# RG-LRU steps issued two at a time, with a ring of four convolution buffers, in a hybrid decoder trunk

## The reference

```python
u = conv_b; u = u + xc[:, j:j+L] * conv_w[j]          # causal convolution, j = 0..3
r  = sigmoid(u @ w_a + b_a); ig = sigmoid(u @ w_i + b_i)   # block-diagonal weights
log_a = LRU_C * r * log_sigmoid(lam)
a  = exp(log_a)
bt = sqrt(-expm1(2 * log_a)) * ig * u
h_t = a_t * h_{t-1} + bt_t                            # scan along the sequence
o_lru = h_seq * gelu(gate)
```

## Time and profile before

| | us |
|---|---|
| median of the 2 runs shown | 4967.77 |
| the two runs | 4776.38 and 5159.16 |
| the profiled execution | 4762.55 |
| its span on the slowest core | 4761.5 |
| spans of the 8 cores in it | 4717.6 to 4761.5 |

### The profile page before, as it was taken

One profiled execution on the slowest core, in us unless ns is written; L12 is line 12 of the kernel. 1 busy time (PEld: TensorE's weight loads), 2 busy tenths in 40 slices (PEclk: granted clock), 3 DMA queues, 4 the chain that ended last, 5 costly groups with the idle time before them and its releaser, 6 DMA issues.

```text
span 4761.5 us, 61283 instructions; the slowest of 8 cores (4717.6 to 4761.5 us)
## 1 busy us (share of the span) xinstructions
PE 3698.8 (78%) x18520; PEld 1598.8 (34%) x18520; DVE 1870.8 (39%) x3170; ACT 1877.3 (39%) x3420; POOL 1318.3 (28%) x1687
## 2 busy tenths in 40 slices
PE   5578976579965799757895778976798778976797
PEld 2223432234422244322342223422243223422243
DVE  3544146441354512454413543146413543146413
ACT  4553236442264521455322552246412552246411
POOL 2503125121243211350312413134212413134212
PEclk9768988579986799866897868987798868987798
DMA  5214421224223054220444204422142304522143
GB/s 109 30 28 65 70 44 27 38 36 70 43 49 47 6 82 61 41 29 10 68 69 113 37 13 73 73 36 33 29 76 46 55 11 73 74 36 33 29 76 78
DMA packets 178574, 239.80 MB, mean 50 GB/s; under 512 B 76880, under 2 KB 79440, under 8 KB 178000
## 3 DMA queue, kind: packets, MB, share of 16 engines
q0 software_dynamic: 129312, 205.77, 28.6%
q1 hardware_dynamic: 48944, 30.12, 2.5%
HBM read 431.16 MB, written 18.51 MB: 94 GB/s over the span
## 4 chain that ended last, share of the span: by engine, by line
PE 58%; DVE 12%; ACT 10%; issue 8%; POOL 7%; DMA 4%; ACTq 0%; DVEq 0%; SPq 0%; POOLq 0%
PE P L345 50%; DVE arena L464 3%; POOL x L382 3%; PE P L692 3%; DVE tmpa L380 3%; PE P L361 2%; ACT sq L359 2%; DVE act L372 1%; DMA arena<-cache_v 1%; ACT arena L700 1%; POOL arena L499 1%; ACT arena L660 1%; DMA x<-xT_in 1%; DVE arena L487 1%; POOL tmpb L609 1%
## 5 line engine op out<-in xcount | busy, mean ns | idle before, releaser
L345 PE MATMUL P<-act,wsl 128*128 128x512 bf16 (+1 forms) x11520 | 2235.0, 358 | 120.6 <-ACT tmpb L608 58.1
L345 PEld LDWEIGHTS P<-act,wsl 128*128 128x128 bf16 x11520 | 1027.6, 102 | 1322.6 <-issue 320.3
L905 DVE TENSOR_TENSOR H<-P,tmpb 128x512 bf16<-128x512 f32 (+1 forms) x440 | 262.0, 601 | 1305.8 <-PE P L345 1138.6
L382 POOL TENSOR_TENSOR x<-x,tmpa 128x512 f32<-128x512 f32 (+1 forms) x320 | 390.3, 1238 | 1282.1 <-DVE tmpa L380 1097.7
L345 PE MATMUL P<-H,wsl 128*128 128x512 bf16 (+1 forms) x3520 | 644.8, 346 | 14.4 <-DMA wsl<-w_down_u 14.4
L903 ACT ACTIVATE tmpb<-P 128x512 f32<-128x512 f32 (+1 forms) x440 | 231.2, 525 | 1006.9 <-PE P L345 1006.8
L361 PE MATMUL P<-sq,ones 128*128 128x512 bf16 (+1 forms) x720 | 290.9, 446 | 363.3 <-ACT sq L359 344.9
L345 PEld LDWEIGHTS P<-H,wsl 128*128 128x128 bf16 x3520 | 302.5, 99 | 349.6 <-issue 22.7
L380 DVE SCALAR_TENSOR_TENSOR tmpa<-F,prm_sb,rstd 128x512 f32<-128x512 f32 (+1 forms) x320 | 287.8, 933 | 256.6 <-POOL x L382 127.2
L464 DVE SCALAR_TENSOR_TENSOR arena<-F,prm_sb,arena 128x512 f32<-128x512 f32 (+1 forms) x240 | 266.2, 1109 | 196.0 <-ACT arena L461 178.0
L359 ACT ACTIVATE sq<-F 128x512 bf16<-128x512 f32 (+1 forms) x400 | 193.5, 548 | 338.3 <-PE P L361 199.9
(11 more groups left out here) (134 smaller groups left out, 3252.9 us busy)
## 6 DMA issues: line engine op xcount, KB each, us to landing
wsl<-w_gate_u POOLq DMA_DIRECT2D x176, 256.0 KB, 4.1
wsl<-w_up_u POOLq DMA_DIRECT2D x176, 256.0 KB, 4.8
wsl<-w_down_u POOLq DMA_DIRECT2D x128, 352.0 KB, 4.8
wsl<-w_in_u POOLq DMA_DIRECT2D x168, 256.0 KB, 4.6
wsl<-w_out_u POOLq DMA_DIRECT2D x64, 256.0 KB, 4.3
x<-xT_in SPq DMA_DIRECT2D x32, 256.0 KB, 12.8
yT<-x SPq DMA_DIRECT2D x16, 512.0 KB, 2.8
sk_old<-cache_k SPq DMA_DIRECT2D x4, 992.0 KB, 7.4
```

Of the source, the lines that this page charges most:

```text
L345: S.op("pe", lambda e, lt=lt, rh=rh, j=j: e.matmul(out_ap, lhsT=lt, rhs=rh, start=(j == 0), stop=(j == n - 1)), reads=rk, writes=[out_key] ...
L382: S.op("pool", lambda e: e.tensor_tensor(x[:, c, lo_:hi_], x[:, c, lo_:hi_], tmpa[j][:, 0:n], ALU.add), reads=akeys("x", [c], s, lo_, hi_) ...
L905: S.op("dve", lambda e: e.tensor_tensor(H[:, c, lo_:hi_], P[bu_][:, 0:n], tmpb[j][:, 0:n], ALU.mult), reads=[pk(bu_), ("tmpb", j)], writes ...
```

## The change

`u32` and `u16` get a fourth buffer. `lru_A` loses its square root, which becomes a function of its own, `lru_S`, and can leave out the cast of the next step. `lru_advance` issues two steps in one call, ahead of every third slot, with `lru_B` of a step ahead of `lru_A` of the step two later. Ahead of the first slot four `lru_pre` stand instead of two, and two `lru_A` instead of one.

```diff
-        u32 = [av(3072 + 512 * i, 512) for i in range(3)]
-        u16 = [av(4608 + 256 * i, 256, BF16) for i in range(3)]
+        u32 = [av(3072 + 512 * i, 512) for i in range(4)]
+        u16 = [av(5120 + 256 * i, 256, BF16) for i in range(4)]
...
-                      if k + 1 < len(lsteps):
+                      if cast_next and k + 1 < len(lsteps):
                           lru_cast(k + 1, *lsteps[k + 1])
                       S.op("dve", lambda e: e.scalar_tensor_tensor(lt1[:, 0:n], lt3[:, 0:n], 1.0, lt3[:, 0:n], ALU.min, ALU.mult),
                            reads=[k3, k1], writes=[k1])
+
+                  def lru_S(k, lo_, hi_, c):
+                      n = hi_ - lo_
+                      lt1, k1 = lt[k % 2][0], ("lt1", k % 2)
                       S.op("act", lambda e: e.activation(lt1[:, 0:n], lt1[:, 0:n], AF.Sqrt, scale=-0.25, bias=q25[:]),
                            reads=[k1, "q25"], writes=[k1])
...
                   def lru_advance(nsteps):
-                      for _ in range(nsteps):
-                          k = lstate["k"]
-                          if k >= len(lsteps):
-                              return
-                          lo_, hi_, c = lsteps[k]
-                          if k + 2 < len(lsteps):
-                              lru_pre(k + 2, *lsteps[k + 2])
-                          if k + 1 < len(lsteps):
-                              lru_A(k + 1, *lsteps[k + 1])
-                          lru_B(k, lo_, hi_, c)
-                          lstate["k"] = k + 1
+                      ns = len(lsteps)
+                      while nsteps > 0 and lstate["k"] < ns:
+                          j = lstate["k"]
+                          lru_B(j, *lsteps[j])
+                          if j + 2 < ns:
+                              lru_A(j + 2, *lsteps[j + 2], cast_next=True)
+                          if j + 1 < ns:
+                              lru_B(j + 1, *lsteps[j + 1])
+                          if j + 3 < ns:
+                              lru_A(j + 3, *lsteps[j + 3], cast_next=False)
+                          for d in (2, 3):
+                              if j + d < ns:
+                                  lru_S(j + d, *lsteps[j + d])
+                          for d in (4, 5):
+                              if j + d < ns:
+                                  lru_pre(j + d, *lsteps[j + d])
+                          if j + 4 < ns:
+                              lru_cast(j + 4, *lsteps[j + 4])
+                          lstate["k"] = min(j + 2, ns)
+                          nsteps -= 2
...
-                  lru_pre(0, *lsteps[0])
+                  for d in range(4):
+                      lru_pre(d, *lsteps[d])
                   lru_cast(0, *lsteps[0])
-                  lru_pre(1, *lsteps[1])
-                  lru_A(0, *lsteps[0])
+                  lru_A(0, *lsteps[0], cast_next=True)
+                  lru_A(1, *lsteps[1], cast_next=False)
+                  lru_S(0, *lsteps[0])
+                  lru_S(1, *lsteps[1])
+                  lru_cast(2, *lsteps[2])
...
-                          lru_advance((len(lsteps) * nqk) // (6 * len(tiles)) - lstate["k"])
+                          tgt = ((len(lsteps) // 2) * nqk) // (6 * len(tiles)) * 2
+                          lru_advance(tgt - lstate["k"])
```

More of the change, by code:

```diff
@@ L258, in build_program @@
                     + [("pTc", h, g) for h in range(2) for g in range(4)] + [("pTn", h) for h in range(2)] + ["esr"])
-        LRU_KEYS = ([(nm, i) for nm in ("lt1", "lt2", "lt3") for i in range(2)] + [(nm, i) for nm in ("u32", "u16") for i in range(3)])
+        LRU_KEYS = ([(nm, i) for nm in ("lt1", "lt2", "lt3") for i in range(2)] + [(nm, i) for nm in ("u32", "u16") for i in range(4)])
         def fence(wait_keys, set_keys):
@@ L445, in lru_pre @@
                       n = hi_ - lo_
-                      uu, ub = u32[k % 3], u16[k % 3]
-                      uk, ubk = ("u32", k % 3), ("u16", k % 3)
+                      uu, ub = u32[k % 4], u16[k % 4]
+                      uk, ubk = ("u32", k % 4), ("u16", k % 4)
                       cw = lambda j: prm[:, l, 40 + 4 * c + j:41 + 4 * c + j]
@@ L468, in lru_cast, with lru_A @@
                       n = hi_ - lo_
-                      S.op("act", lambda e: e.copy(u16[k % 3][:, 0:n], u32[k % 3][:, 0:n]), reads=[("u32", k % 3)], writes=[("u16", k % 3)])
-                  def lru_A(k, lo_, hi_, c):
+                      S.op("act", lambda e: e.copy(u16[k % 4][:, 0:n], u32[k % 4][:, 0:n]), reads=[("u32", k % 4)], writes=[("u16", k % 4)])
+                  def lru_A(k, lo_, hi_, c, cast_next=True):
                       n = hi_ - lo_
@@ L474, in lru_A @@
                       k1, k2, k3 = ("lt1", k % 2), ("lt2", k % 2), ("lt3", k % 2)
-                      ub, ubk = u16[k % 3], ("u16", k % 3)
+                      ub, ubk = u16[k % 4], ("u16", k % 4)
                       for wi, bank in ((0, 4), (1, 5)):
@@ L495, in lru_B @@
                       k1, k2, k3 = ("lt1", k % 2), ("lt2", k % 2), ("lt3", k % 2)
-                      uu, uk = u32[k % 3], ("u32", k % 3)
+                      uu, uk = u32[k % 4], ("u32", k % 4)
                       S.op("dve", lambda e: e.scalar_tensor_tensor(lt2[:, 0:n], lt2[:, 0:n], 1.0, uu[:, 0:n], ALU.add, ALU.mult),
```

## The result

**Slower, by the mechanism forecast.** The changed kernel takes 1.0609 times as long as the kernel before (95% interval 1.0564 to 1.0655). The profiled execution took 5060.9 us, with a span of 5059.9 on its slowest core, again core 6. The forecast was 5090, in a range from 4920 to 5250. The medians of all runs (5179.62 of 11 after, 4787.13 of 10 before) hold executions in which one die ran at a lower clock, so the ratio is taken without those.

The account below looks back on a forecast made before the run. Eight stretches, 825.9 us, were taken as bound by a chain between engines, with DVE's queue setting the pace. Longer stretches add 4 x 30.1 + 4 x 52.6 = +331 us to 4762.6, giving 5093, said as 5090, range 4920 to 5250.

Parts of the forecast that it names:

- The removal: ACT's table loads at square roots and tanhs: 80 loads of 1.283 us go, 102.6 us of ACT.
- The chain, step by step: One full pair of steps becomes one chain: period 32.9 us for 21.57 (second pass), 30.3 for 19.34 (first).
- POOL's pile: Three L609 and L611 pile up on POOL, then three weight DMAs to 33.7 us, before the next product.
- The ends: Starts and ends of the eight stretches: with the periods, 123.9 us for 93.8 (second pass), 165.2 for 112.6 (first).
- The sum: All eight stretches: 4 x 30.1 + 4 x 52.6 = +331 us, saved table loads already taken out.
- not shown: How DVE and POOL overlap in the 24 full periods and 16 ends: -64 to +160 us.
- The signs: Changed profile: loads near 80, PE waits of 7 to 10 and 4 us per pair, stretches near 165 and 124 us.
- DVE's queue sets the pace: Kernel before, pair of steps: DVE busy 17.55 of 21.57 us, with two waits for POOL of 1.58.
- Milder: Rival, chance 0.17: POOL's pile does not form, period 27.7 us in the second pass, total 4938.
- DVE keeps the pace: Rival, chance 0.10: saved loads pay for longer hand-offs, a pair still takes 21.6 us, total 4760, within 2%.
- Faster: Rival, chance 0.06: ACT's loads are the place, a pair falls under 21.6 us, total 4660.
- Steeper: Rival, chance 0.07: DVE and POOL meet in nearly every instruction, PE slow in each slot, total 5250 to 5330.

Follow-up runs that it names:

- the last version: Three-lt-set version (one step per call, paired square roots, early product) with scan and POOL's two instructions behind it issued after the following slot: 0.9963 of the kernel before.

## Why the prediction was right, and which terms were off

**The removal.** 80 loads of 1.283, 102.6 us of ACT, were predicted and are gone. ACT fell by 102.3 in the stretches. In the kernel before the loads lay beside other work: 152 of them are worth about 18 us (the same edit on the kernel before). That the forecast charged one load in and one back to the chain was half wrong: the one ahead of the tanh is covered, since the second tanh waits for POOL anyway. The forecast's period is not touched by that: with the load in place L527 is done about when the second tanh wants to start, as it said.

**The chain, step by step.** With t = 0 at 4026.25, 0.8 before the product as the forecast had it:

| step | forecast | measured |
|---|---|---|
| L477 of j + 3 | 7.7 | 7.5 |
| exp of j + 3 ends | 14.2 | 14.1 |
| ACT done with square roots and L461, L464 starts | 17.7 | 17.6 |
| first bank copy ends | 21.5 | 21.2 |
| third slot ends | 26.8 | 26.4 |
| next product | 33.7 | 33.1 |

The period is 30.95 and 32.29 where 32.9 was said. The difference lies in POOL's pile: its first L629 ended at 25.3 (4051.52), forecast 26.1; and POOL issued two weight DMAs in the shorter period (1.13) and four in the longer (1.13 and 1.12), where three in each (1.7) were put. The pairs behind it took 2.7 to 3.0, as forecast. The first pass had 29.41 and 29.94 for 30.3. That the shared `lt` closes the chain is shown by the third set, which takes two thirds of the loss back.

**The ends.** Second pass: the second L477 of the start came 9.33 after the gate matmuls, forecast 9.6; the stretch is 120.7 to 121.3 for 123.9. First pass: the first cast came 9.59 after the stretch's start (forecast 731.1 - 721.4 = 9.7) and the stretch is 160.9 to 163.4 for 165.2. But the size put on that start was wrong as a *cause*: undone, it gives about 3.3 us of the 7.4, because the next wait of PE grows. Whoever adds such a delay in full overstates it.

**The sum.** +305.8 for +331, 25 too high: 12 in the second passes, of which the periods make 10 (4 x (65.8 - 63.2)), and 13 in the first, of which they make 5 (4 x (60.6 - 59.35)) and the ends the rest. The term that was called not shown, DVE beside POOL, came out mild: six L464 took 5.66, where twice the short form is 4.92. Its bounds were -64 and +160.

**The signs.** The forecast named a wait of 7 to 10 us ahead of the second L477 of a pair and one of 4 for the bank copy. In the four full periods of the two stretches read here they were 9.1 to 13.0 and 4.8 to 7.8. The first was set too low by the forecast's own chain: with the third slot done at 26.8 and the next L477 at 32.9 + 7.7 = 40.6, less the 0.6 of the two matmuls of j + 2, PE stands for 13.2. The loads are 72 (40 and 32), not 80: the tanhs at the start of each of the eight stretches follow no square root.

**What bounded the kernel before.** "DVE's queue sets the pace" was too simple. One of three L464 less gave 28 us of 82, an earlier product 15, and no load 18; POOL's work moved behind the rotary made it slower. The waits of DVE for POOL and of POOL for DVE in these runs suggest that the two set the pace together. No run relieved both at once, so how it divides between them stays open.

**The rivals.** *Milder* asked that POOL's pile not form: POOL stands idle for 8.75 us and then works through its pile, with one wait of 1.29, from 4047.65 until the product ends at 4060.60. *DVE keeps the pace* would have the period at 21.6: 31 to 32. *Faster* asked for tanhs that don't wait for the scan of j; even given a third set, the order in pairs stays 2.1% slower. *Steeper*: PE had clock 0.53 in the first half of the third slot and 1.00 after it, not the lower level throughout.

## What to carry to other kernels

Before grouping operations to save a fixed cost, ask whether the fixed cost is on the path, and draw the cycle that the grouping makes through the buffers: with two buffer sets and steps issued two at a time, the second step's inputs wait for the first step's outputs, and every engine stands in one line. Compare the busy time of each engine in the stretch with its length; when they fall and the stretch grows, look for the buffer or the queue position that closes the chain, and add a set before changing the order. A wait removed at one place in such a chain comes back at the next (90 us at the bank copy, of which 67 came back ahead of L477).

## What the runs showed of the hardware

- A table load took 1283 ns, and the operation behind it started 1.30 after the load's start (4040.39 to 4041.69). Taking both loads of a period away shortened it by 1.35, with one of them covered, so nothing beyond the load's own time hung on it here. The Trainium skill (ScalarE: Activation LUTs, "What ACT_TABLE_LOAD costs") puts a switch at 2.66 us with a drain; no run here shows the drain.
- DVE and POOL slow each other by large factors: three L464 took 2.46 alone, 4.93 in the kernel before and 6.39 in the last version; the scan 1.28 and 2.14; POOL's addition 1.26 and 2.11. The Trainium skill (GPSIMD Engine Reference, "Specifications") says that GpSimd shares its SBUF interfaces with VectorE; these rows agree. An order that keeps them apart saved DVE 94 us of L464 (266.2 to 171.9) and still lost, since the time was spent waiting.
